# One product of each output group is done as two of 144 columns: a decoder trunk in fp32 pairs on one core

## What is computed

```python
def swiglu(h, w_in, w_out):
    g, u = jnp.split(h @ w_in, 2, axis=-1)
    return (jax.nn.silu(g) * u) @ w_out
...
        x = x + rms_norm(m, g[1])
        f = swiglu(rms_norm(x, g[2]), ffn_w_in[li], ffn_w_out[li])
        x = x + rms_norm(f, g[3])
```

## Time and profile before

| what | value |
|---|---|
| median of 3 runs | 1504.8 us (1504.06 to 1506.75) |
| the profiled execution | 1504.36 us, of which 1502.8 us is the span from first to last instruction |
| TensorE products (PE) | 1480.4 us busy, 99% of the span, 10818 of them |
| weight loads (PEld) | 1463.6 us busy |
| VectorE (DVE), ScalarE (ACT) | 1031.4 us (69%), 708.7 us (47%) |
| mean granted TensorE clock | 0.997 of full speed, that is the upper one of its levels |

### The profile page before, as it was taken

How to read it: one execution, slowest core, us unless ns; L and a number is a source line. 1 busy time by engine, 2 the same in 40 slices (tenths; PEclk the granted TensorE clock), 3 DMA queues, 4 the chain that set the end, 5 groups by cost and what they waited for, 6 DMA issues and landing times.

```text
span 1502.8 us, 28251 instructions
## 1 busy us (share of the span) xinstructions
PE 1480.4 (99%) x10818; PEld 1463.6 (97%) x10818; DVE 1031.4 (69%) x1624; ACT 708.7 (47%) x1115; POOL 91.3 (6%) x93
## 2 busy tenths in 40 slices
PE   7999999999999999999999999999999999999997
PEld 7999999999999999999999999999999999999996
DVE  6454577667344689998973538968689988974435
ACT  5344332324343465555553535685565555553423
POOL 0100033333000000000000000000000000000003
PEclk9999999999999999999999999999999999999998
DMA  7312232323232223343342232313222333322311
GB/s 238 112 63 69 85 111 84 96 87 101 71 99 85 71 57 85 84 112 84 84 139 72 89 95 58 112 40 101 71 68 60 101 95 84 111 94 91 99 29 67
DMA packets 170508, 133.49 MB, mean 89 GB/s; under 512 B 4888, under 2 KB 147504, under 8 KB 170292
## 3 DMA queue, kind: packets, MB, share of 16 engines
q1 hardware_dynamic: 168756, 128.30, 28.9%
q0 software_dynamic: 1664, 3.95, 0.9%
HBM read 128.92 MB, written 3.29 MB: 88 GB/s over the span
## 4 chain that ended last, share of the span: by engine, by line
PE 93%; DVE 4%; issue 1%; ACT 1%; DMA 0%; POOL 0%; SPq 0%; ACTq 0%; DVEq 0%
PE ps L546 67%; PE ps L836 26%; DVE acc L1365 1%; DVE xT L1629 1%; DVE wide L1620 1%; DVE yb L1620 0%; DVE wlo L1688 0%; DMA wide<-in_x_prompt_dram 0%; DVE hl L1396 0%; PE ps L616 0%; POOL xT L2058 0%; DVE xT L1624 0%; ACT rb L989 0%; PE ps L941 0%; DVE ffg L1546 0%
## 5 line engine op out<-in xcount | busy, mean ns | idle before, releaser
L546 PE MATMUL ps<-hh,whi 128*128 128x288 f32 x2112 | 556.7, 297 | 1.8 <-DVE ffg L1546 0.9
L546 PE MATMUL ps<-hh,wlo 128*128 128x288 f32 x2112 | 551.0, 294 | 0.0
L546 PE MATMUL ps<-hl,whi 128*128 128x288 f32 x2112 | 550.0, 294 | 0.0
L546 PEld LDWEIGHTS ps<-hh,whi 128*128 128x128 f32 x2112 | 372.5, 188 | 4.1 <-issue 2.4
L546 PEld LDWEIGHTS ps<-hl,whi 128*128 128x128 f32 x2112 | 372.3, 188 | 0.5
L546 PEld LDWEIGHTS ps<-hh,wlo 128*128 128x128 f32 x2112 | 372.5, 188 | 0.0
L1348 DVE TENSOR_TENSOR wlo<-stage,whi 128x1024 fp32r<-128x1024 f32 (+2 forms) x168 | 191.2, 1144 | 221.1 <-ACT whi L959 220.7
L959 ACT ACTIVATE whi<-stage 128x1024 fp32r<-128x1024 f32 (+2 forms) x168 | 165.6, 994 | 361.6 <-PE ps L546 351.2
L836 PE MATMUL ps<-shi,whi 128*128 128x288 f32 x576 | 169.9, 295 | 2.0 <-ACT acc L1197 2.0
L836 PE MATMUL ps<-slo,whi 128*128 128x288 f32 x576 | 170.3, 296 | 0.0
L836 PE MATMUL ps<-shi,wlo 128*128 128x288 f32 x576 | 170.2, 296 | 0.0
(11 more groups left out here) (196 smaller groups left out, 2025.3 us busy)
## 6 DMA issues: line engine op xcount, KB each, us to landing
stage<-in_ffn_w_in_dram SPq DMA_DIRECT2D x88, 512.0 KB, 4.1
stage<-in_ffn_w_out_dram SPq DMA_DIRECT2D x40, 512.0 KB, 4.4
stage<-in_gm_w_in_dram SPq DMA_DIRECT2D x32, 384.0 KB, 3.6
stage<-in_gm_w_in_dram SPq DMA_DIRECT2D x24, 512.0 KB, 3.8
stage<-in_gm_w_out_dram SPq DMA_DIRECT2D x24, 512.0 KB, 3.8
stage<-in_rg_w_in_dram SPq DMA_DIRECT2D x16, 512.0 KB, 4.1
stage<-in_rg_w_out_dram SPq DMA_DIRECT2D x8, 512.0 KB, 3.9
wide<-in_x_prompt_dram SPq DMA_DIRECT2D x2, 1024.0 KB, 7.2
```

Of the source, the lines that this page charges most:

```text
L546: return pe.matmul(out, w, x, start=start, stop=stop)
```

## The change

`three` has a new argument. Where it is set, the third product of the six (the first half, high weights, `hl`) is done as two products of 144 columns into the two parts of the same bank. `out_phase` sets it for the first product block of each group (unit 0, kk 0, m 0) of every output stage but RO. That is six places in the execution: two groups in each of GO, FO0 and FO1. Nothing else is different: the same columns, the same weights, the same sums, no other wait and no other transfer.

```diff
-            def three(m, hi_w, lo_w, k, first, last):
+            def three(m, hi_w, lo_w, k, first, last, odd=False):
 
                 a, b = ps[:, 2 * m, 0:HT], ps[:, 2 * m + 1, 0:HT]
                 mm(a, hi_w, hh[:, k, 0:HT], first, False)
                 mm(b, hi_w, hh[:, k, HT:TT], first, False)
-                mm(a, hi_w, hl[:, k, 0:HT], False, False)
+                if odd:
+                    for at in (slice(0, HT // 2), slice(HT // 2, HT)):
+                        mm(ps[:, 2 * m, at], hi_w, hl[:, k, at], False, False)
+                else:
+                    mm(a, hi_w, hl[:, k, 0:HT], False, False)
                 mm(b, hi_w, hl[:, k, HT:TT], False, False)
...
-                                last = three(m, *weights(first + j, kk, m), 2 * (j % 4) + kk, j == 0 and kk == 0, False)
+                                last = three(m, *weights(first + j, kk, m), 2 * (j % 4) + kk, j == 0 and kk == 0, False,
+                                             odd=(j, kk, m) == (0, 0, 0) and name != "RO")
```

## The result

The changed kernel takes 1509.21 us in the median of 11 runs (1508.29 to 1510.19), against 1504.64 us (1504.03 to 1506.75, 11 runs). The ratio is 1.0029 with a 95% interval of 1.0021 to 1.0037: slower by 3.2 to 5.6 us.

What follows compares the result with a forecast made beforehand. TensorE, busy 99% of the span, was taken as the bound. Groups 0 turning fast gave 4.4 us, minus direct cost 0.1, so 1504.8 - 4.3 = 1500.5 us; range 1499.6 to 1505.5.

Steps and rivals of the forecast that it cites:

- Two forms of one stream: Alternating a, b products in TensorE's stream: slow 133.3 ns or fast 130.0 ns, set by the entry and kept.
- 3.33 ns a product: Gain from slow to fast in groups 0: 1.60 us in GO, 1.44 us each in FO0 and FO1.
- The split exchanges them: First split gives b, not a, the even place; groups 0 of GO, FO0, FO1 turn fast, together 4.48 us.
- parity: Whether a or b has the even place in TensorE's stream; exchange held likelier than not in GO, about even in FO0, FO1.
- The second split, at its beginning, turns it back: Split at the start of group 1 undoes the exchange, so groups 1 keep 130.0 ns instead of being slow.
- The objection that I wrote down and passed over: Groups 0 and 1 have the same parity, 480 + 96 products apart, yet different forms, so parity alone isn't the state.
- Rival 2: Splits spoil the fast groups 1 and don't mend groups 0: 3.5 us, with direct cost 3.7, 1508.5 us; chance 0.13.
- The direct cost: Splitting a product at the six places adds 17 ns each, for six +0.1 us (0.08 to 0.8).
- The waits in FO0 and FO1: Two short waits following the split in groups 0 of FO0 and FO1 may set the state anew.
- The DMA share of fast GO: Group 1 of GO: put at 0.36 against 0.30 in slow GO, to show DMA doesn't sort the forms.
- Some 20 products that gain nothing: First products of each slow stretch in GO, FO0 and FO1 don't take part, lowering the gain from 4.48 to 4.4 us.

Runs made afterwards that it cites:

- b first: Kernel before, with each block of the alternating part of GO, FO0 and FO1 taking b first and a second, all products whole; 1507.92 us, ratio 1.0021.
- the first kernel with runs: Kernel before, without splits; fourth unit of group 0 of GO, FO0 and FO1 done as 24 products of a, then 24 of b; 1505.18 us, ratio 1.0006.

## Why the prediction was wrong, step by step

- **Two forms of one stream, set at its entry and kept.** Right, and each run shows it: 130.0 or 133.3 ns over whole stretches, and no load of another engine sorts them. The number of 3.33 ns a product is right as well; three groups 1 with 1056 products lost 3.5 us of the 3.86.
- **"The split exchanges them. In group 0 that turns slow into fast."** This is the step that failed. I had made parity, the places of a and b, the likeliest meaning of the hidden state, because the trace had no odd block to speak against it. In mid-stream an odd split, a missing product and an even pair of splits all leave a slow stream slow and make a fast one slow. A disturbance doesn't exchange, it resets, and the stream was slow behind each of the eighteen places of these three kernels (the six of the changed kernel, six without the product, six in mid-stream; in four of them, the groups 0 of FO0 and FO1 in the first two, a wait lies in between).
- **"The second split, at its beginning, turns it back."** There was nothing to turn back; the second splits were the ones that cost, 3.7 us of time without the first ones.
- **The objection that I wrote down and passed over.** Groups 0 and 1 stand at equal parity and differ in form. That excluded parity as the state; I noted that "the runs of a and b between them also change it" and didn't follow it. It was the true mechanism: one run of a and one of b turn the form over, in all 20 places where such runs were put behind a settled alternation. What they hand on is a place in a period of four products, and a count by twos can't name it. The starts in the trace of the kernel before had this period, and I had read only means. It had stood in the rows as well, slow group 0, two runs, fast group 1, three times of three.
- **Rival 2** (0.13) was what happened, with its place and nearly its size: 3.5 us plus direct cost, 3.7, against 3.86 in the trace. Its reason, a break two products behind a smooth passage, holds. But "a short product counts as a break" was too narrow, since a missing one and b first do the same.
- **The direct cost.** I took 17 ns a split, bounded by 13 and 133; it is about 90. The error was to price each half by the nearest spacing of small products. The product behind the pair is late as well, which a list of equal products doesn't show. In the first group 1 of the changed kernel two halves and the product behind them have 65, 110 and 178 ns, where two products of a fast stream have 260. Over the six stretches it makes 3.86 - 3.52 = 0.34 us. The rule of the Trainium skill ("TensorE: Matmul & The Clock Gate", section "Back-to-back issue gap"), 81 ns for 128 columns, was nearer with 29 ns and still below the measured 90. No row of that kind stands for 144 columns in a stream of their own, so the page's figure itself is not tested here. Its lack of a second form at one size is contradicted in every run.
- **The waits in FO0 and FO1** "may set the state anew": right. The same code behind the same wait was slow in the kernel before and fast in two of the kernels tried, and the sequence of starts differed by a few ns only. In the changed kernel both groups 0 were slow behind that wait.
- **Smaller slips.** The DMA share of fast GO is 0.33 over the stretch, not 0.36. Some 20 products that gain nothing in each of three stretches take 0.2 us from 4.48, not 0.1. Neither moves the forecast by more than 0.1.

What stays open: why the two forms exist, and where the period of four comes from. A stream of a alone had 131.7 ns and of b alone 133.3 in every kernel, which an explanation would have to give too. Nor did any run decide whether a group 1 that begins with b can be entered fast, or what a wait has to look like to leave a fast stream.

## What to carry to other kernels

Where a kernel is bound by TensorE, divide long uniform stretches of the trace by their products. Two spacings at one size and one clock mean a state that can be lost or won without changing any work. Before guessing what sets such a state, list every stretch with the form ahead and behind it; here that list of seven already named the runs between the groups. Read a few single starts of each form as well: the mean of 133.3 ns hid one long spacing in four. And a fast stretch can be a thing of its entry: leave alone what stands at its beginning, since one product split in two there cost 1.2 us in the 336 behind it.

## What I had not expected of the hardware

- Products of 288 columns at the upper clock, with a weight load each, have 130.0 or 133.3 ns when two column halves alternate, 131.7 for the first half alone and 133.3 for the second alone.
- The form is kept over 480 products and turned over by 12 products of a and 12 of b, in this order. The slow form has one spacing of 140 ns in four, the fast one none.
- After a wait of 0.1 to 0.2 us the form differed where the starts differed by a few nanoseconds. In the kernel before, the third unit of FO0 began with 0.34 us from its first pair to its second (776.68 to 777.02) and stayed slow; with this entry of the first kernel with runs, 0.01 us longer, it became fast:

```profile
776.59 0.43 PE L546 MATMUL ps<-hh,wlo 128*128 128x288 f32 x2
776.99 0.51 PE L546 MATMUL ps<-hh,whi 128*128 128x288 f32 x2
777.34 0.42 PE L546 MATMUL ps<-hl,whi 128*128 128x288 f32 x2
```

- The time from the first instruction to the first output stage varied by 1.9 us (358.92 to 360.79) between executions whose code is equal up to there, about as much as half the effect. The lengths of stages in the trace agreed to 0.02 us and told the small effects apart where the times couldn't.
